# Feed forward with the high and the low part of the rows in one matmul of 512 columns

## The reference

```python
D_FF = 2816

def swiglu(h, w_gate, w_up, w_down):
    return (jax.nn.silu(h @ w_gate) * (h @ w_up)) @ w_down

    for l in range(2):          # first_block
        ...                     # mixer, cross attention
        h = rms_norm(x, pre_ffn_g[l])
        x = x + rms_norm(swiglu(h, w_gate[l], w_up[l], w_down[l]), post_ffn_g[l])
```

## Time and profile before

| | us |
|---|---|
| median of 3 runs | 2262.33 (2260.16 to 2262.98) |
| profiled execution | 2261.26 |
| its span | 2259.5 |
| TensorE busy | 1798.4 (80%) |
| VectorE busy | 814.3 (36%) |
| ScalarE busy | 529.3 (23%) |
| feed forward of layer 0, first matmul to last | 261.8 to 454.9 |
| feed forward of layer 1 | 681.6 to 874.7 |
| stream of the experts' weights | from 939.8 |

### The profile page before, as it was taken

One profiled execution on the slowest core, in us unless ns is written; L12 is line 12 of the kernel. 1 busy time (PEld: TensorE's weight loads), 2 busy tenths in 40 slices (PEclk: granted clock), 3 DMA queues, 4 the chain that ended last, 5 costly groups with the idle time before them and its releaser, 6 DMA issues.

```text
span 2259.5 us, 28736 instructions
## 1 busy us (share of the span) xinstructions
PE 1798.4 (80%) x12614; PEld 1156.2 (51%) x12614; DVE 814.3 (36%) x1237; ACT 529.3 (23%) x797; POOL 88.2 (4%) x136
## 2 busy tenths in 40 slices
PE   8999999999999999998755666666766566666576
PEld 7899999999889998863211111111222111221111
DVE  5855677767667776841100100100010010010101
ACT  5745534456444334630000000000000000000000
POOL 1200000012100000000000000000000000000000
PEclk9999999999999999999888877887887886887878
DMA  8345667754546775599999999999999999999997
GB/s 266 128 162 187 193 224 242 238 160 156 190 155 213 244 246 174 200 396 426 431 428 430 429 428 431 428 429 430 428 429 428 429 429 429 429 429 430 429 429 316
DMA packets 172077, 739.80 MB, mean 327 GB/s; under 512 B 6784, under 2 KB 133248, under 8 KB 146992
## 3 DMA queue, kind: packets, MB, share of 16 engines
q1 hardware_dynamic: 169600, 731.27, 81.5%
q0 software_dynamic: 2352, 6.69, 0.9%
HBM read 736.88 MB, written 1.05 MB: 327 GB/s over the span
## 4 chain that ended last, share of the span: by engine, by line
DMA 49%; PE 41%; DVE 5%; ACT 3%; issue 1%; POOL 0%; SPq 0%; DVEq 0%; POOLq 0%; ACTq 0%
PE PS L369 40%; DMA WB<-in_w_up 24%; DMA WB<-in_w_down 24%; DVE WL L1722 2%; ACT WH L1169 1%; DVE S L1717 1%; DVE X L1717 1%; DMA W<-in_w_gate 0%; PE PS L468 0%; POOL T L2572 0%; DMA W<-in_w_in 0%; DVE S L1714 0%; DVE HTl L1717 0%; ACT HTh L1230 0%; DVE CN L1714 0%
## 5 line engine op out<-in xcount | busy, mean ns | idle before, releaser
L369 PE MATMUL PS<-WB,XS 128*32 128x352 f32 x3360 | 393.0, 628 | 243.3 <-DMA WB<-in_w_up 163.0
L369 PEld LDWEIGHTS PS<-WB,XS 128*32 128x32 f32 x3360 | 124.8, 139 | 509.2 <-DMA WB<-in_w_up 219.0
L1722 DVE TENSOR_TENSOR WL<-W,WH 128x2048 fp32r<-128x2048 f32 x138 | 317.0, 2297 | 142.2 <-ACT WH L1169 142.2
L1717 DVE SCALAR_TENSOR_TENSOR S<-S,PS 128x352 f32<-128x352 f32 (+1 forms) x110 | 63.3, 588 | 750.3 <-PE PS L369 420.2
L369 PE MATMUL PS<-WB,S 128*32 128x512 f32 (+1 forms) x1204 | 235.0, 732 | 116.2 <-DMA WB<-in_w_down 93.5
L1169 ACT ACTIVATE WH<-W 128x2048 fp32r<-128x2048 f32 x141 | 269.6, 1912 | 198.5 <-PE PS L369 193.2
L369 PE MATMUL PS<-HTh,WH 128*128 128x256 f32 x1064 | 306.9, 288 | 8.8 <-DVE HTl L1717 5.5
L369 PE MATMUL PS<-HTl,WH 128*128 128x256 f32 x1064 | 301.5, 283 | 0.0
L369 PE MATMUL PS<-HTh,WL 128*128 128x256 f32 x1064 | 301.5, 283 | 0.0
L369 PEld LDWEIGHTS PS<-HTh,WH 128*128 128x128 f32 x1064 | 204.3, 192 | 13.9 <-DVE WL L1722 6.8
L369 PEld LDWEIGHTS PS<-HTl,WH 128*128 128x128 f32 x1064 | 204.5, 192 | 0.8
(11 more groups left out here) (283 smaller groups left out, 2166.2 us busy)
## 6 DMA issues: line engine op xcount, KB each, us to landing
WB<-in_w_up SPq DMA_DIRECT2D x63, 2816.0 KB, 36.4
WB<-in_w_gate SPq DMA_DIRECT2D x47, 2816.0 KB, 35.7
WB<-in_w_down SPq DMA_DIRECT2D x46, 2816.0 KB, 36.0
CN<-in_w_gate SPq DMA_DIRECT2D x16, 2816.0 KB, 36.7
CN<-in_w_down SPq DMA_DIRECT2D x16, 2816.0 KB, 36.3
W<-in_w_in SPq DMA_DIRECT2D x31, 1024.0 KB, 5.4
S<-in_w_ada SPq DMA_DIRECT2D x24, 1024.0 KB, 5.3
W<-in_w_gate SPq DMA_DIRECT2D x22, 1024.0 KB, 7.9
```

Source lines behind the costliest of these rows:

```text
L369: return e.matmul(o, l, r, start=start, stop=stop, skip_group_check=True)
L1717: return e.scalar_tensor_tensor(out=o, in0=a, scalar=s, in1=b, op0=o1, op1=o2)
L1722: e.tensor_tensor(M.WL[i][:, :], M.SLOT[m % NW], M.WH[i][:, :].bitcast(F32), ALU.subtract).then_inc(*up("low", m))
```

## The change

The high and the low part of the rows become one tile `HT2`, [128, 2, 8, 256], of which `HT[0]` and `HT[1]` are the halves. `gate` and `up` are made by a new `proj_halves`: for each half j and chunk k one matmul of 512 columns (weights' high part stationary, high and low rows moving, in two pieces that lie 2048 elements apart) and one of 256 columns (weights' low part, high rows) into the first 256. So half j fills a bank of its own: `gate` has banks 0 and 1 of the four, `up` 2 and 3, and `ada_sum` always bank 3, all by the new `given`. The two column ranges of a bank have to be added: ScalarE copies the second ranges of both banks into `FG` or `FU` (`halves`, 128x512), VectorE adds the first ranges (two operations of 128x256), which frees the banks; tanh and the products then read `FG` and `FU`.

The order by hand changes with it: ScalarE and VectorE split the next round's `up` ahead of `f_hi` and of the product's low part. In round 1 both skip their first `unit()`, and VectorE begins with `ada_sum` and the gate's sums and makes all four adaLN steps behind them, ahead of the split of the next `up`.

```diff
--- before.py
+++ after.py
@@ -256,7 +256,8 @@
         M.S = sb("S", [128, 10240], F32, first)
         M.BD = sb("BD", [128, 4, 128], F32, first)
         M.MEM = [sb(n, [128, 8, 256], F32R, first) for n in ("MEMh", "MEMl")]
-        M.HT = [sb(n, [128, 8, 256], F32R, first) for n in ("HTh", "HTl")]
+        M.HT2 = sb("HT", [128, 2, 8, 256], F32R, first)
+        M.HT = [M.HT2[:, i] for i in range(2)]
         M.W = sb("W", [128, 2048 * NW], F32, first)
 
         M.SLOT = [M.W[:, 2048 * i:2048 * i + 2048] for i in range(NW)]
@@ -317,6 +318,7 @@
     M.TMP2, M.XS0 = view(8192, 2, 1024), view(7680, 8, 32)
     M.CV, M.CK = M.XN, N1[:, 2048:4096].rearrange("p (a b) -> p a b", a=8)
     M.A = [view(512 * i, 2, 256) for i in range(2)]
+    M.FG, M.FU = view(1024, 2, 256), view(1536, 2, 256)
     M.AK = view(2048, 8, 128)
     M.AS = [M.AK[:, :, 32 * i:32 * i + 32] for i in range(4)]
     M.AW = [view(3072 + 2048 * i, 8, 256) for i in range(2)]
@@ -355,6 +357,12 @@
 
     def take(name, hold=False):
         i, k = C.banks.take(name, hold)
+        if k > 1:
+            e.wait_ge(C.sig.sem(f"bank{i}"), k - 1)
+        return PS[:, 4 + i, :]
+
+    def given(name, i):
+        i, k = C.banks.give(name, i)
         if k > 1:
             e.wait_ge(C.sig.sem(f"bank{i}"), k - 1)
         return PS[:, 4 + i, :]
@@ -395,6 +403,23 @@
             beside.step()
         drop(to)
         same(("full", *to), ("unit", m))
+
+    def proj_halves(name, l, n, to, b, norm=None):
+
+        m, u = unit(name, l, "cols", n)
+        for j in range(2):
+            ps = given((*to, j), b + j)
+            for k in range(8):
+                if norm and j == 0:
+                    e.wait_ge(*at("lo", norm, k))
+                w = part(u, slice(None), k, slice(128 * j, 128 * j + 128))
+                mm(two(ps), w[0], M.HT2[:, :, k, :], k == 0, False)
+                ins = mm(ps[:, 0:256], w[1], HT[0][:, k, :], False, k == 7)
+            if j:
+                ins.then_inc(*up("unit", m))
+            beside.step()
+        for j in range(2):
+            same(("full", *to, j), ("unit", m))
 
     def proj_r(name, l, n, src, to, off=0):
 
@@ -507,7 +532,7 @@
         e.wait_ge(*at("ada_acc", n))
         if sec in (3, 4) and j < 3:
             return
-        ps, acc, ones = take(("ada", n)), products(i, M), M.CST[:, C_ONES:C_ONES + 128]
+        ps, acc, ones = given(("ada", n), 3), products(i, M), M.CST[:, C_ONES:C_ONES + 128]
         if sec in (2, 5):
             ins = mm(ps[:, 0:256], ones, acc, True, True)
         elif sec in (3, 4):
@@ -781,9 +806,9 @@
             same(("down", l, n), ("unit", m))
 
         for n in range(11):
-            proj_t("w_gate", l, n, HT, ("g", l, n), norm=("ffn", l) if n == 0 else None)
+            proj_halves("w_gate", l, n, ("g", l, n), 0, ("ffn", l) if n == 0 else None)
             ada_sum(12 * l + n)
-            proj_t("w_up", l, n, HT, ("u", l, n))
+            proj_halves("w_up", l, n, ("u", l, n), 2)
             if n > 1:
                 down(n - 2)
             if n < 10:
@@ -1503,19 +1528,34 @@
         unit()
 
     def ffn(l):
+        def halves(o, what, l, n, b):
+            full(what, l, n, 1)
+            if n:
+                e.wait_ge(*at("f_prod", l, n - 1))
+            e.activation(o, PS[:, 4 + b:6 + b, 256:512], ACT.Copy).then_inc(*up("f_half", what, l, n))
+
         for n in range(11):
             A, i = M.A[n % 2], n % 4
+            if n != 1:
+                unit()
             unit()
-            unit()
-            g = two(full("g", l, n))
-            if n >= 2:
-                e.wait_ge(*at("hid", l, n - 2))
-            e.activation(flat(A), flat(g), ACT.Tanh, scale=0.5).then_inc(*up("f_tanh", l, n))
+            halves(M.FG, "g", l, n, 0)
             if n > 1:
                 unit()
             else:
                 early()
-            e.wait_ge(*free("u", l, n))
+            if n >= 2:
+                e.wait_ge(*at("hid", l, n - 2))
+            for j in range(2):
+                e.wait_ge(*free("g", l, n, j))
+            e.activation(flat(A), flat(M.FG), ACT.Tanh, scale=0.5).then_inc(*up("f_tanh", l, n))
+            halves(M.FU, "u", l, n, 2)
+            if n:
+                early()
+            else:
+                unit()
+                early()
+            e.wait_ge(*at("f_prod", l, n))
             if n < 4:
                 e.wait_ge(*at("y", "cross", l))
             else:
@@ -2228,22 +2268,43 @@
         for n in range(11):
             A, i = M.A[n % 2], n % 4
             job = modulation(12 * l + n + 1) if n else iter(range(4))
-            unit()
-            next(job)
-            ada_sum(12 * l + n)
-            unit()
-            next(job)
-            g, u = flat(two(full("g", l, n))), flat(two(full("u", l, n)))
-            e.wait_ge(*at("f_tanh", l, n))
-            stt(flat(A), flat(A), 1.0, g, ALU.add, ALU.mult).then_inc(*freed("g", l, n))
+
+            def halves(o, what):
+                e.wait_ge(*at("f_half", what, l, n))
+                for j in range(2):
+                    e.tensor_tensor(o[:, j, :], full(what, l, n, j)[:, 0:256], o[:, j, :], ALU.add).then_inc(*freed(what, l, n, j))
+
+            if n == 1:
+                ada_sum(12 * l + n)
+                halves(M.FG, "g")
+                unit()
+                next(job)
+                next(job)
+            else:
+                unit()
+                next(job)
+                ada_sum(12 * l + n)
+                unit()
+                next(job)
+                halves(M.FG, "g")
             next(job)
             if n > 1:
                 unit()
             next(job)
             if n < 2:
                 early()
-            e.wait_ge(*free("g", l, n))
-            stt(flat(A), flat(A), 0.5, u, ALU.mult, ALU.mult).then_inc(*freed("u", l, n))
+            halves(M.FU, "u")
+            e.wait_ge(*at("f_tanh", l, n))
+            stt(flat(A), flat(A), 1.0, flat(M.FG), ALU.add, ALU.mult).then_inc(*step())
+            own()
+            for j in range(2):
+                e.wait_ge(*free("u", l, n, j))
+            stt(flat(A), flat(A), 0.5, flat(M.FU), ALU.mult, ALU.mult).then_inc(*up("f_prod", l, n))
+            if n:
+                early()
+            else:
+                unit()
+                early()
             e.wait_ge(*at("f_hi", l, n))
             e.tensor_tensor(MX[1][:, 2 * i:2 * i + 2, :], A, MX[0][:, 2 * i:2 * i + 2, :].bitcast(F32), ALU.subtract).then_inc(
                 *up("hid", l, n))
```

## The result

The changed kernel takes 2267.04 us in the median (2262.97 to 2269.61), the kernel before 2262.51 us (2260.13 to 2264.50), 20 runs of each: ratio 1.0019 [1.0013, 1.0026], 4.5 us or 0.2% slower. I had forecast 2258.6 us with a range up to 2265.0. The time lies outside the range, and the direction was wrong too: the matmuls did become cheaper, though by half of what I had worked out, and the waits, with the slow clock behind them, cost more than twice as much.

The account below looks back on a forecast made before the run. TensorE's matmul pace was taken to bound both feed-forward stages. Layer 0 gains 4.2 + 0.5 - 2.0 = 2.7 us, layer 1 4.2 - 3.2 = 1.0, together 3.7: 2258.6 us against the 2262.33 median, range 2252.5 to 2265.0.

Parts of the forecast that it names:

- 42 units with wide matmuls: `gate` and `up`, 21 of 22 units per layer: each 0.20 us shorter, 8.4 us less for both layers.
- late `up` starts in layer 0: Three late rounds where `up` started 0.29 instead of 0.12 after the previous matmul: mended by the earlier split, 0.5 us gained.
- wait in `up`(1), layer 0: `up`'s second half in round 1 waits for bank 3 until VectorE has read the adaLN column: 2.0 us.
- wait before `up`(2), layer 1: TensorE waits 2.65 us for VectorE's first `up` sum, behind all four adaLN steps; 2.3 us more than before.
- wait before `down`(0), layer 1: TensorE waits for the split weights of `down`(0), queued behind `f_hi`(1): another 0.9 us.
- What bounds the kernel: Both feed-forward stages are TensorE's; time won there starts the experts' weight stream earlier and should reach the end whole.
- Banks: `gate` needs what VectorE freed a round earlier.: Steady rounds: the step checking PSUM banks for `gate`; it gave no added wait.
- the pair: One 512-column and one 256-column matmul in `gate` or `up`: 0.228 + 0.120 = 0.348 us, instead of 0.360.
- number (4): Rival: 512 columns are not faster between matmuls of 256; half the gain, waits as said, 2262.8 us; chance 0.11.
- Rival (1): Clock falls behind round 1's waits; layer 0 loses 1 to 1.7 us, layer 1 almost nothing; 2260.3 us; chance 0.18.
- Rival (2): Round 1's waits are absent, VectorE or ScalarE reaching steps otherwise than ordered; gain 9.5 us, 2252.8 us; chance 0.12.
- Rival (3): TensorE pays 12.5 ns for each piece of the moving operand; the 8.4 us go, waits stay; 2267.0 us; chance 0.09.

Follow-up runs that it names:

- e1: The changed kernel with banks swapped: `gate` in 2 and 3, `up` in 0 and 1, adaLN sum in 1; 2262.61 us.
- e5: The changed kernel with the edits of e1 and e3, and round 1's adaLN column read ahead of the next `gate` split; 2256.89 us.
- e10: e5 with each half's 512-column matmuls ahead of its 256-column ones, except the half waiting for the norm's rows; 2255.06 us.
- e3: The changed kernel with two of the four adaLN steps of layer 1's round 1 done in round 0; 2264.08 us.
- e4: The changed kernel with the rows' high and low parts side by side, so the 512 moving columns are contiguous; 2267.67 us.
- e9: The changed kernel with six unused matmuls put into the wait before `gate`(0) of layer 0, the wait itself kept; 2265.64 us.

## Why the prediction was wrong, point by point

| step | forecast, us | measured, us |
|---|---|---|
| 42 units with wide matmuls | -8.4 | 42 x 0.11 = -4.6 |
| late `up` starts in layer 0 | -0.5 | gone, as said |
| wait in `up`(1), layer 0 | +2.0 | +2.0 |
| wait before `up`(2), layer 1 (more than before) | +2.3 | 2.9 less 0.34: +2.6 |
| wait before `down`(0), layer 1 | +0.9 | 0, covered by the slow clock |
| wait before `gate`(0), layer 0 | none | 4.03 less 1.56: +2.5 |
| slow clock behind the three idle times | none | +2.1, +1.7, about +1.3 |

The last term of the last row holds the wait before `down`(0), some 0.7 us by e1.

The terms measured add up to +7.1 us; the stream shows +5.2. Of the rest, 0.5 us is that the transposes came that much earlier in this run (259.69 against 260.23), 0.5 us is given back between `down`(0) and `up`(3) of layer 1 (+7.22 to +6.77), and some 0.5 us lies in layer 0's `up` units behind the adaLN matmuls, which gained more than 0.11 (5.83 a unit before, now 5.63). The last 0.4 us I can't place.

- **What bounds the kernel** was right. The stream of the kernel after starts 5.2 us later and the median is 4.5 higher; those of e5 and e10 start 5.0 and 7.3 us earlier than before and their medians are 5.6 and 7.6 lower. Single spans follow only within the 3 us told above.
- **The failed step** is the sentence "Banks: `gate` needs what VectorE freed a round earlier." It holds from round 1 on. For round 0 I never asked who had used bank 0 last, and the wait before `gate`(0) stood in my sum with nothing. The last user was a `k` product that ScalarE reads behind the norm; with banks in turn, `gate` had met another one. The wait and its slow clock are the 4.4 us that e1 gives back. Without them the change would have been even with the kernel before, inside the range, though still above my number.
- **The mis-sized term** is the pair: 0.3525 us instead of 0.348. I took the price of a 512-column matmul among its like (0.228) for one between matmuls of 256 columns, where it costs 0.3525 - 0.120 = 0.233 in a `gate` unit. My bounds for the term, 0.2155 and 0.240, did hold it. I had a rival with half the gain, number (4), and for the gain it was right. Its reason was another: in e10 the same matmuls and weight loads, grouped, give the whole 0.20 us in a `gate` unit (5.56), so what took part of it back is the order. Whether the 12.5 ns are the matmul's or its weight load's no run tells, since each matmul here has one. The rule that I had weighed, the Trainium skill's "TensorE: Matmul & The Clock Gate", section "Back-to-back issue gap", would have each matmul cost only 2.5 ns beyond its columns and the pair save as little. A pair saved 7 ns alternating and 12 grouped (0.3595 less 5.56/16 = 0.3475), and single steps leave some 13 ns, so the rows decide against it here; but for the pair as the change has it the rule came out nearer than I did (2.5 and 12.5 against 7).
- **The two forecast waits** came with their place, releaser and size: 2.0 and 2.9 us against 2.0 and 2.65. VectorE's added sums took 0.67 us a pair (708.03 to 708.70) against my 0.7. The third, before `down`(0), shows in e1 and e3 with 0.7 to 0.8 against 0.9. The order of the steps on VectorE, written out by hand and costed by row, was worth the work.
- **Rival (1), the clock,** was right in its mechanism, though its 2260.3 us was 6.7 too low. I had put the price at 1 to 1.7 us in layer 0 (1.7 measured behind the wait it spoke of; the 2.1 at `gate`(0) hang on the missed wait) and almost nothing in layer 1, which was near: of about 1.3 us some 0.7 stand for the wait before `down`(0), and in five other profiled kernels the clock didn't fall there at all. What I had held against it, that 2.0 us is shorter than both rows of before, was no argument: here the clock fell behind 1.84 us of idle time. The Trainium skill describes in the same page, section "A second HAM failure mode: psum-queue depth-cycling", that short idle times of TensorE, which come back at each turn through the PSUM banks, make the clock swing. This trace shows it of a single one: 0.64 behind an idle time of 1.84 us that a PSUM bank caused.
- **Rival (2)**, no waits in round 1, fell with the rows. **Rival (3)**, two pieces, fell with e4, though its 2267.0 us is what was measured: the right time by a wrong cause.
- **Adding independent errors.** Half the gain (+3.8) and the clock were rivals by themselves, and my range took them one at a time; the missed wait was in none. They came together, and all three pushed the same way.

What stays open: why an alternating pair costs 0.3525 us directly behind `down` and 0.347 behind the adaLN matmuls, why grouping helps the first and not the second, and why the clock fell behind an idle time of 2.76 us in one kernel and not behind the same one in five others.

## What to carry to other kernels

Where a change turns buffers taken in turn into fixed ones, look up for each the last reader ahead of the stage, not only in the steady loop; the first round is where a reader from another stage is still in the way, and another number for the buffer can be all the cure (4.4 us here). Cost a wait of TensorE of some 2 us and more with the slow clock behind it as a risk, up to 2 us more, and don't judge it by one trace. Ask of each edit that frees TensorE time whether VectorE's queue still meets it. Where wide and narrow matmuls can be grouped, try it and measure it unit by unit: it gained 0.08 us in `gate` units and lost 0.04 in layer 0's `up` units, and where a producer paces the wide ones the narrow ones had better stay in the gaps.

## What the runs showed of the hardware

- The order of matmuls of different widths changes their price: 16 pairs of 512 and 256 columns behind `down` take 5.64 us alternating and 5.56 us in groups of eight. Behind four matmuls of one column it is 5.63 alternating and 5.67 grouped.
- A moving operand of two pieces, 2048 elements apart, costs the same as a contiguous one: 5.64 us a unit with either.
- The granted clock fell behind an idle time of 1.84 us in five of six profiled kernels, behind the one of 2.76 us in one of six, and behind the one of 2.99 us in all five that left TensorE idle there. Where it fell in the kernel after, TensorE lost 2.7 us (e9 beside after), some 1.7 and some 1.3.
- Matmuls whose result nobody uses, put into an idle time of 3 us, left the clock at 1.00 behind it in the one execution profiled (e9: 36 matmuls in 5.9 us instead of 19 in 6.0).
